# Reordering the expert tiles of a routed MoE stage, with the routing weights' table and the late gate rows moved on TensorE and VectorE

## The chip, the cores and the metric

One Trainium2 chip, one core of it. The metric is the device time of one execution in microseconds. The kernel is one program for one transformer-like layer in 32-bit floats. Its engines are TensorE (PE, with weight loads listed as PEld), VectorE (DVE), ScalarE (ACT), GpSimd (POOL) and SyncE (SP), which only issues DMAs here.

## The reference

640 tokens (512 latent, 128 context) of width 1024 pass through modulation, a gated convolution and a differential attention, a merge with an output projection (result `x`), and then the stage that this case is about:

```python
h2 = rms_norm(x, norm2_g) * (1 + scale2) + shift2
x = x + gate2 * hier_moe(h2, ...)          # gate2 differs for latent and context tokens

def hier_moe(t):                            # 16 experts, each token goes to 2 of them
    for e in range(16):
        he = silu(t @ w1[e]) * (t @ w3[e])  # 1024 -> 512, twice
        y = y + combine[:, e:e + 1] * (he @ w2[e])   # 512 -> 1024
    return y
```

`combine` holds the two routing weights of each token (a softmax over its two experts, times its group's probability).

## The kernel before

Each expert's three matrices (w1 "gate", w3 "up", w2 "down") are 2 MB each, so 48 loads of 2 MB pass through the core once. The experts are sorted on the chip by how many tokens they have. Rank r of that order is read by SP with `expert_at(r)`. Slots for the sorted tokens are packed in twelve output tiles of 128 rows:

- A **couple** t (0 to 5, `t < WHOLE`) joins a large expert `a` (rank 7 - t, 96 rows) with a small expert `b` (rank 8 + t, 32 rows). Its main tile needs both experts' matrices: TensorE works in four strips of 32 rows, three with a's matrix and one with b's.
- Tiles t = 6 and 7 are whole tiles: 128 rows of one large expert (rank 1 and rank 0), so they need only a's matrices.
- A **half tile** holds 64 more rows of one small expert `b`. Two of them (for t = 2j and 2j + 1) make output tile `half j`. So there are 8 half-tile gate/up steps (`half_gate_up`) and 4 joint down steps (`half_down`).

For every main tile TensorE runs `main_gate`, `main_up`, `half_gate_up`, then three blocks of transposes (`hidden_T`, `next_tokens`, `half_hidden_T`) and `main_down`; after an odd t also `next_tokens` and `half_down`. The order of the twelve outputs before is: 0, 1, half 0, 2, 3, half 1, 4, 5, half 2, 6, half 3, 7. In the tail half_down(3) stands behind five of the eight steps of tile 7's gate product.

In the traces these are the lines L2428 (gate and up of a couple), L2430 (of a whole tile), L2452 and L2453 (gate/up of a half tile), L2490 and L2492 (down of a couple and of a whole tile), L2504 (down of a half tile), L2462 (`hidden_T`), L2394 (`next_tokens`) and L2470 (`half_hidden_T`).

The engines pass the work on with semaphores, and every order is written out by hand:

- SP loads matrices into six gate/up buffers and three down buffers (`GU_UNIT`, `DOWN_UNIT`), in the order of the tiles. Before it loads over a buffer it waits for the product that read it (`s_gate_mm`, `s_up_mm`, `s_half_mm`, `s_d`).
- POOL gathers the tokens of the next tiles from `h2` in device memory (three buffers), and adds finished rows onto `y_sample` and `y_prompt` in device memory. A couple's tile and a joint half tile take two such adds each (their strips have rows in common), a whole tile takes one. Each add waits for the one before it.
- ACT copies transposes out of PSUM and computes silu. `tokens_T` copies a tile's transposed tokens.
- DVE multiplies silu by up and by the slot's routing weight (`hidden`, `hidden_half`), makes the row gates of an output tile (`slot_gates(n)`, into one of two buffers `gated`) and multiplies the down product by them (`rows_made(n)`). `slot_gates(n)` waits until the adds of outputs up to n - 2 have landed. Before the change it stands directly behind `rows_made(n - 1)`, which is ahead of the next `hidden`.

Work that leads into the stage: the last tile's h2 is written to device memory by ACT's queue, the slots' token numbers come from `table(i)` on TensorE, the slots' routing weights from `weight_table(i)` (five token tiles, L2406, each needs two one-hot blocks made by DVE), and the last modulation product (`ada_part(LAST_PAIR, ...)`, 8 steps) gives gate2: its product is copied by ACT (`late_rows`), transposed by TensorE (L2509), corrected by DVE, transposed once more (L2517), stored by ACT's queue and read back by POOL's queue as rows `gate2`. DVE turns those into a difference with `gate_difference` (L1874) before the first `slot_gates`.

```python
def slot_gates(n, tile):
    if n >= 2:
        added = 16 * sum(adds_before[m] for m in range(n - 1))
        dve.wait_ge(s_put_lat, added)
        dve.wait_ge(s_put_ctx, added)
```

Of the kernel before, what the change touches and what calls it, by code (L numbers as in the profile page):

```python
# [7 lines left out]
P = 128  # L8
# [214 lines left out]
TOKEN_TILES = [col for t in range(COUPLES) for col in ((t,) if t % 2 else (t, COUPLES + t // 2))]  # L223
XG = 3


def out_main(t):

    return t + t // 2 if t + 1 < COUPLES else TILES - 1


def out_half(j):

    return 3 * j + 2 if j + 1 < QUADS else TILES - 2


def gate_up_units():

    unit = {}
    for t in range(COUPLES):  # L240
        unit[("gate", "a", t)] = unit[("gate", "b", t - 2)] if t >= 2 else 4 * t
        unit[("gate", "b", t)] = unit[("up", "b", t - 2)] if t >= 2 else 4 * t + 1
        unit[("up", "a", t)] = unit[("gate", "a", t - 1)] if t else 2
        unit[("up", "b", t)] = unit[("up", "a", t - 1)] if t else 3
    return unit


def down_units():

    unit = {("a", 0): 0, ("b", 0): 1, ("a", 1): 2, ("b", 1): 0}  # L250
    for t in range(2, COUPLES):
        first, second = (("b", "a") if t + 1 == COUPLES else ("a", "b"))
        unit[(first, t)] = unit[("a", t - 1)] if t % 2 == 0 else unit[("b", t - 2)]
        unit[(second, t)] = unit[("b", t - 2)] if t % 2 == 0 else unit[("a", t - 1)]
    return unit
# [3 lines left out]
GU_LOADS = [(part, which, t) for t in range(COUPLES)  # L259
            for part, which in ((("gate", "b"), ("gate", "a"), ("up", "b"), ("up", "a")) if t + 1 == COUPLES  # L260
                                else (("gate", "a"), ("gate", "b"), ("up", "a"), ("up", "b")))]
DOWN_LOADS = [(which, t) for t in range(COUPLES) for which in ("ba" if t + 1 == COUPLES else "ab")]
# [22 lines left out]
def build(nc, io):  # L285
# [4 lines left out]
    with ExitStack() as ctx:  # L290
# [279 lines left out]
        def _(sp):  # L570
# [100 lines left out]
            for t in range(COUPLES - 1):  # L671
                a, b = expert_at(COUPLES - 1 - t), expert_at(COUPLES + t)
                if t == 1:
                    sp.wait_ge(s_late, 1)
                if t >= 2:
                    sp.wait_ge(s_half_mm, t - 1)
                load_gate_up("gate", "a", t, a)
                if t == 0:
                    job_done(sp, "wo", 2 * NT - 1)
                load_gate_up("gate", "b", t, b)  # L680
                if t:
                    sp.wait_ge(s_gate_mm, t)
                load_gate_up("up", "a", t, a)
                if t:
                    sp.wait_ge(s_up_mm, t)
                else:
                    sp.wait_ge(s_xg[0], 16)
                    sp.wait_ge(s_outx, 16 * NT)
                load_gate_up("up", "b", t, b)
                if t == 0:  # L690
                    sp.wait_ge(s_x2, 2 * NT)
                    sp.wait_ge(s_last_scaled, 1)
                elif t == 1:
                    sp.wait_ge(s_wtable, NT)
                elif t % 2:
                    sp.wait_ge(s_d, 2 * out_half(t // 2 - 1) + 2)
                elif t:
                    sp.wait_ge(s_d, 2 * out_main(t - 1) + 2)
                load_down("a", t, a)
                if t % 2:  # L700
                    sp.wait_ge(s_d, 2 * out_main(t - 1) + 2)
                elif t:
                    sp.wait_ge(s_d, 2 * out_half(t // 2 - 1) + 2)
                load_down("b", t, b)
            t = COUPLES - 1
            a, b = expert_at(0), expert_at(EXPERTS - 1)
            sp.wait_ge(s_half_mm, t - 1)
            load_gate_up("gate", "b", t, b)
            load_gate_up("gate", "a", t, a)
            sp.wait_ge(s_up_mm, t)  # L710
            load_gate_up("up", "b", t, b)
            load_gate_up("up", "a", t, a)
            sp.wait_ge(s_d, 2 * out_half(t // 2 - 1) + 2)
            load_down("b", t, b)
            sp.wait_ge(s_d, 2 * out_main(t - 1) + 2)
            load_down("a", t, a)

# [21 lines left out]
        def _(pool):  # L739
# [166 lines left out]
            for t in range(COUPLES - 1):  # L906
                add_main(t)
                gather_next(XG + 2 + out_main(t))
                if t % 2:
                    add_half(t // 2)  # L910
                    gather_next(XG + 2 + out_half(t // 2))
            add_half(QUADS - 1)
            add_main(COUPLES - 1)
# [27 lines left out]
        def _(act):  # L941
# [240 lines left out]
            def hidden_T(n):  # L1182
                act.wait_ge(s_HT, n + 1)
                if n:
                    act.wait_ge(s_d, 2 * out_main(n - 1) + 2)
# [10 lines left out]
            A(late_rows, late_psum, ACT.Copy).then_inc(s_late_rows, 1)  # L1196
            tokens_T(0)
# [4 lines left out]
            A(unused[:, 2:3], ones[:, 0:1], ACT.Silu)  # L1202
            tokens_T(1, half=True)
            for t in range(COUPLES - 2):
                silu_main(t)
                silu_half(t)
                hidden_T(t)
                tokens_T(2 + out_main(t))
                half_hidden_T(t)
                if t % 2:  # L1210
                    tokens_T(2 + out_half(t // 2), half=True)
            t = COUPLES - 2
            silu_main(t)
            silu_half(t)
            hidden_T(t)
            tokens_T(TILES - 1)
            half_hidden_T(t)
# [1419 lines left out]
```

## Time and profile before

| | us |
|---|---|
| median of 3 runs | 1212.82 (1210.62 to 1213.5) |
| profiled execution, its own time | 1208.31 |
| span of the profiled execution | 1206.5 |
| TensorE busy | 1159.9 (96%) |
| VectorE, GpSimd, ScalarE busy | 537.2, 354.2, 226.2 |
| chain that ended last: PE, DMA, DVE | 78%, 14%, 2% of the span |
| DMA | 201.89 MB, mean 167 GB/s over the span |
| 48 expert matrices | 2048 KB each |

The table is of one execution. The span is what the profiler saw between the first and the last instruction. The expert stage is the last quarter of it: the first expert matrix is asked for at about 885 us and the last add lands at 1206. Busy time says which engine works, not which one sets the end. A matmul in 32-bit floats is listed as two instructions.

### The profile page before, as it was taken

What the parts mean: (1) busy time and instruction counts of PE and PEld (TensorE: products, weight loads), DVE (VectorE), ACT (ScalarE), POOL (GpSimd) and SP (SyncE); (2) the same over time, 40 slices, a digit from 0 to 9 for tenths busy, and PEclk for the clock granted to TensorE, in tenths of its full rate; (3) what the DMA queues carried; (4) which work ended last, traced back from release to release, by engine and by line L of the source; (5) the groups of instructions that cost most, each with busy time, mean ns of one, the idle gap of its engine ahead of it and who ended that gap; (6) DMA issues with size and microseconds to landing.
All of it is one profiled execution on the core that took longest, in us unless ns stands there. A gap on an engine that the chain in (4) does not pass through costs nothing.

```text
span 1206.5 us, 14503 instructions
## 1 busy us (share of the span) xinstructions
PE 1159.9 (96%) x5750; PEld 710.2 (59%) x5751; DVE 537.2 (45%) x1045; ACT 226.2 (19%) x478; POOL 354.2 (29%) x289
## 2 busy tenths in 40 slices
PE   4899999999999999999999999999988999999995
PEld 1567677677777777777777777765543333333332
DVE  2553369365596675275324433545583211211121
ACT  3221247322473001100110011002121111111010
POOL 0465600277103233233333333200001123322323
PEclk9999999999999999999999999999987999999999
DMA  9944320022200222222212223541169999999982
GB/s 353 328 150 164 114 79 1 18 71 79 79 1 1 71 70 71 70 70 70 70 70 70 70 70 142 227 170 72 58 251 361 413 407 409 410 401 411 400 321 28
DMA packets 53988, 201.89 MB, mean 167 GB/s; under 512 B 5344, under 2 KB 5920, under 8 KB 47776
## 3 DMA queue, kind: packets, MB, share of 16 engines
q1 hardware_dynamic: 47040, 185.20, 39.6%
q0 software_dynamic: 6272, 14.17, 4.4%
q10 hardware_dynamic: 608, 1.58, 0.3%
q8 instruction: 46, 0.75, 0.2%
q14 instruction: 22, 0.18, 0.0%
HBM read 189.36 MB, written 18.91 MB: 173 GB/s over the span
## 4 chain that ended last, share of the span: by engine, by line
PE 78%; DMA 14%; DVE 2%; issue 1%; ACT 0%; POOLq 0%; POOL 0%; DVEq 0%
PE psum L2252 35%; PE psum L2058 12%; DMA y_sample<-arena,slot_rows 7%; PE psum L2316 6%; PE psum L2160 4%; PE psum L2220 3%; PE psum L2036 3%; DMA y_sample<-arena,slot_rows_b 3%; PE psum L2428 2%; PE psum L1978 2%; PE psum L2452 2%; DMA y_sample<-arena,slot_rows_q 1%; DMA y_prompt<-arena,slot_rows_ctx 1%; PE psum L2194 1%; PE psum L2430 1%
## 5 line engine op out<-in xcount | busy, mean ns | idle before, releaser
L2252 PE MATMUL psum<-arena,weight_ring 128*128 128x320 f32 x928 | 256.9, 432 | 0.0
L2252 PEld LDWEIGHTS psum<-arena,weight_ring 128*128 128x128 f32 x928 | 175.9, 190 | 72.7
L762 POOL TENSOR_TENSOR weight_ring<-weight_ring 128x512 f32<-128x512 f32 x80 | 107.0, 1338 | 352.5 <-DMA weight_ring<-in_w_in 201.4
L2252 PE MATMUL psum<-x,weight_ring 128*128 128x320 f32 x640 | 179.5, 432 | 0.0
L2252 PEld LDWEIGHTS psum<-x,weight_ring 128*128 128x128 f32 x640 | 121.1, 190 | 49.6
L763 POOL TENSOR_TENSOR weight_ring<-weight_ring 128x512 f32<-128x512 f32 x80 | 110.8, 1385 | 0.0
L1537 DVE TENSOR_TENSOR arena<-psum,arena 128x320 f32<-128x320 f32 x124 | 59.5, 488 | 92.1 <-PE psum L2252 91.4
L2058 PE MATMUL psum<-weight_ring,x 128*128 128x256 f32 x384 | 88.3, 380 | 0.5 <-DVE x L1294 0.5
L2428 PE MATMUL psum<-weight_ring,arena 128*32 128x512 f32 x512 | 78.6, 609 | 1.1 <-ACT arena L1167 1.1
L2058 PEld LDWEIGHTS psum<-weight_ring,x 128*128 128x128 f32 x384 | 71.6, 190 | 11.7 <-DVE x L1294 1.3
L2316 PE MATMUL psum<-weight_ring,arena 128*128 128x512 f32 x160 | 71.8, 596 | 0.0
L2058 PE MATMUL psum<-weight_ring,arena 128*128 128x256 f32 x288 | 67.5, 381 | 0.0
L1537 DVE TENSOR_TENSOR arena<-psum,ropeC 128x320 f32<-128x320 f32 x40 | 19.6, 491 | 102.3 <-PE psum L2252 102.0
L1132 ACT ACTIVATE ropeC<-psum 128x320 f32<-128x320 f32 x28 | 12.2, 437 | 263.7 <-PE psum L2252 246.7
L2058 PEld LDWEIGHTS psum<-weight_ring,arena 128*128 128x128 f32 x288 | 53.3, 190 | 10.8 <-issue 4.3
L1905 DVE SCALAR_TENSOR_TENSOR arena<-arena,ropeC 128x1024 f32<-128x1024 f32 x12 | 15.4, 1282 | 84.0 <-DMA y_prompt<-arena,slot_rows_b_ctx 62.8
L1088 ACT ACTIVATE arena<-psum,softmax_stats 128x640 f32<-128x640 f32 x64 | 50.5, 792 | 7.4 <-DVE softmax_stats L1462 7.4
L1462 DVE TENSOR_REDUCE softmax_stats<-psum 128x2 f32<-128x1280 f32 x32 | 47.7, 1490 | 6.6 <-PE psum L2160 6.4
L946 ACT ACTIVATE arena<-psum 128x512 f32<-128x512 f32 (+1 forms) x49 | 26.9, 552 | 122.2 <-PE psum L2073 59.5
L2316 PEld LDWEIGHTS psum<-weight_ring,arena 128*128 128x128 f32 x160 | 29.3, 190 | 31.2 <-issue 31.1
L1913 DVE TENSOR_TENSOR arena<-psum,arena 128x512 f32<-128x512 f32 x24 | 16.5, 691 | 69.3 <-PE psum L2490 36.6
L2160 PE MATMUL psum<-arena 64*128 64x128 f32 (+3 forms) x256 | 46.2, 467 | 0.0
(346 smaller groups left out, 1530.4 us busy)
## 6 DMA issues: line engine op xcount, KB each, us to landing
arena<-in_w SPq DMA_DIRECT2D x22, 2048.0 KB, 17.2
weight_ring<-in_w SPq DMA_DIRECT2D x21, 2048.0 KB, 23.5
weight_ring<-in_w_in SPq DMA_DIRECT2D x16, 2048.0 KB, 8.4
arena<-in_w_ada SPq DMA_DIRECT2D x6, 2048.0 KB, 11.5
x<-in_w SPq DMA_DIRECT2D x5, 2048.0 KB
weight_ring<-in_w_ada SPq DMA_DIRECT2D x8, 1024.0 KB, 14.3
x<-in_x_sample SPq DMA_DIRECT2D x2, 2048.0 KB, 12.2
weight_ring<-in_w_conv_out SPq DMA_DIRECT2D x2, 2048.0 KB, 7.8
```

The costliest lines, as they stand in the source:

```text
L762: nc.gpsimd.tensor_tensor(out[:, 0:2], a_[:, 0:2], b_[:, 0:2], op)
L763: nc.gpsimd.tensor_tensor(out[:, 2:4], a_[:, 2:4], b_[:, 2:4], op).then_inc(signal, 1)
L1088: last = A(prob[n % 2][:, c, :], S[:, KEYS * c:KEYS * (c + 1)], ACT.Exp, bias=st[:, c:c + 1], accum_out=st[:, 4 + c:5 + c])
L1462: V.reduce_max(sm[:, 8 * (n % 4):8 * (n % 4) + 2], S2, axis=AX, negate=True).then_inc(s_max, 1)
L1537: return V.tensor_tensor(out, product_psum(q, name), value, add)
L2036: last = mm(ps[LANE * half:LANE * (half + 1), 0:512], hT[:, k, HALF * half:HALF * half + LANE], w, start=(k == 0), stop=(k == KT - 1))
L2058: last = mm(ps[:, 0:256], x_[:, k, :], w_[:, k, :], start=(k == 0), stop=(k == 3))
L2160: last = mm(psum[:, base + KEYS * c + lo:base + KEYS * c + hi], q, kT[64 * c:64 * (c + 1), h, key:key + hi - lo], start=True, stop=True)
L2220: last = mm(psum[:, lo:lo + P], aT[n % 2][:, P * j:P * (j + 1)], v_sb[:, j, P * h:P * (h + 1)], start=(j == 0), stop=(j == NT - 1))
L2252: last = mm(product_psum(q, name), w[:, k, :], src[:, k, :], start=(k == 0), stop=(k == 3))
L2316: last = mm(ps[:, 0:512], mixT[:, k, P * i:P * (i + 1)], w[:, k, :], start=(k == 0), stop=(k == KT - 1))
L2428: last = mm(out[rows_, :], xgT[:, k, rows_], (b if lane == 3 else a)[:, k, :], start=(k == 0), stop=(k == KT - 1))
```

## The change

It changes orders, and with them the counts that the semaphores wait for. No product and no load is added or dropped.

- **Tiles.** Tile 6 (`FIRST`, the whole tile of rank 1) goes first, without its half tile. Then the couples 0 to 5. Then `half_gate_up(6)`, `half_down(2)`, `main_down(5)`, `half_gate_up(7)`, and tile 7 (`LAST`), with half_down(3) now behind three of the eight steps of its gate product. Outputs: 6, 0, 1, half 0, 2, 3, half 1, 4, half 2, 5, half 3, 7. `before(t)` is the place of main tile t in this order.
- **Loads.** Only gate a, up a and down a of tile 6 come before the first tokens are gathered (before: gate a, gate b, up a of couple 0). The six of couple 0 follow. At the end come gate b and up b of 6 and 7, gate a and up a of 7, then the down matrices b6, b7, a7; both b7 and a7 wait for `main_down(5)`.
- **Ahead of the first tokens.** The late modulation product is cut: steps 2 to 4 before `table`, 5 to 7 behind it. All five `weight_table` blocks stand ahead of the first tokens' transposes. The late product's first transposes stand behind tile 6's gate product, its second behind two steps of the up product; DVE does its part after the expert counts.
- **Gate rows.** `gate_difference` and `slot_gates(0)` stand behind couple 0's `hidden_half`; every later `slot_gates(n)` directly ahead of its own `rows_made(n)`, and for a main tile behind that couple's `hidden_half`.

```diff
+FIRST, LAST = COUPLES - 2, COUPLES - 1
+MAINS = [FIRST] + list(range(WHOLE)) + [LAST]
+TOKEN_TILES = [FIRST, 0, COUPLES, 1, 2, COUPLES + 1, 3, 4, COUPLES + 2, 5, LAST, COUPLES + 3]
+OUT_TILES = [FIRST, 0, 1, COUPLES, 2, 3, COUPLES + 1, 4, COUPLES + 2, 5, COUPLES + 3, LAST]
...
+            load_gate_up("gate", "a", FIRST, first)
+            job_done(sp, "wo", 2 * NT - 1)
+            load_gate_up("up", "a", FIRST, first)
+            sp.wait_ge(s_x2, 2 * NT)
+            sp.wait_ge(s_last_scaled, 1)
+            load_down("a", FIRST, first)
...
+            t = WHOLE - 1
+            sp.wait_ge(s_half_mm, t)
+            load_gate_up("gate", "b", FIRST, small)
+            load_gate_up("up", "b", FIRST, small)
...
+            sp.wait_ge(s_d, 2 * out_half(t // 2) + 2)
+            load_down("b", FIRST, small)
+            sp.wait_ge(s_d, 2 * out_main(t) + 2)
+            load_down("b", LAST, b)
+            load_down("a", LAST, a)
...
@@ DVE
+            hidden(FIRST)
             hidden(0)
             hidden_half(0)
             gate_difference()
-            slot_gates(0, 0)
+            slot_gates(0)
             rows_made(0)
-            slot_gates(1, 1)
...
+            for t in range(WHOLE):
+                if t:
+                    hidden(t)
+                    hidden_half(t)
+                if t + 1 < WHOLE:
+                    slot_gates(out_main(t))
+                    rows_made(out_main(t))
+                    if t % 2:
+                        slot_gates(out_half(t // 2))
+                        rows_made(out_half(t // 2))
...
@@ TensorE
-            ada_part(LAST_PAIR, late_psum, range(2, 8), late_slot).then_inc(s_late, 1)
+            ada_part(LAST_PAIR, late_psum, range(2, 5), late_slot)
             for i in range(NT):
                 table(i)
+            ada_part(LAST_PAIR, late_psum, range(5, 8), late_slot).then_inc(s_late, 1)
...
+            pe.wait_ge(s_order, 1)
+            weight_table(range(NT))
+            next_tokens(0)
+            main_gate(FIRST)
             pe.wait_ge(s_late_rows, 1)
             for t in range(4):
                 last = tr(late_T_psum[:, P * t:P * (t + 1)], late_rows[:, P * t:P * (t + 1)], ident[:, :])
             last.then_inc(s_lateT, 1)
-            pe.wait_ge(s_order, 1)
-            weight_table(range(2))
-            next_tokens(0)
-            main_gate(0)
-            weight_table(range(2, NT))
...
+            main_part(FIRST, "up", up_psum, range(0, 2))
+            pe.wait_ge(s_late_mod, 1)
+            tr(late_rows_psum[0:16, 0:P], rowpack[:, 48:64], ident[:, :]).then_inc(s_late_packT, 1)
+            main_part(FIRST, "up", up_psum, range(2, KT)).then_inc(s_up_mm, 1)
             next_tokens(1)
...
+            hidden_T(FIRST)
+            main_gate(0)
             pe.wait_ge(s_late_copied, 1)
             pe.wait_ge(s_shifted, 1)
-            main_down(0)
...
+            main_down(FIRST)
+            next_tokens(2)
+            for t in range(WHOLE):
+                if t:
+                    main_gate(t)
+                main_up(t)
+                half_gate_up(t)
+                hidden_T(t)
+                next_tokens(3 + t + t // 2)
+                half_hidden_T(t)
+                if t + 1 < WHOLE:
+                    main_down(t)
+                    if t % 2:
+                        next_tokens(5 + 3 * (t // 2))
+                        half_down(t // 2)
+            t = WHOLE - 1
+            next_tokens(5 + 3 * (t // 2))
+            half_gate_up(FIRST)
+            half_down(t // 2)
+            half_hidden_T(FIRST)
+            main_down(t)
+            half_gate_up(LAST)
...
+            main_part(LAST, "gate", gate_psum, range(0, 2))
+            half_hidden_T(LAST)
+            main_part(LAST, "gate", gate_psum, range(2, 3))
             half_down(QUADS - 1)
-            main_part(t, "gate", gate_psum, range(5, KT)).then_inc(s_gate_mm, 1)
...
+            main_part(LAST, "gate", gate_psum, range(3, KT)).then_inc(s_gate_mm, 1)
```

## Rows read from the trace of the kernel before

**Rows 1.** Busy time by stretch: length, then PE, PEld, DVE, ACT, POOL, PEclk, DMA share, GB/s

```profile
910.00:1171.00 261.00, 256.69 (x1743) 94.47 (x1745) 45.89 (x81) 29.24 (x45) 67.86 (x49) 0.99 1.01 404
```

**Rows 2.** TensorE's waits, 905 to 1206 us: total, times, longest

```profile
PE psum L2462 <- DVE arena L1883: 3.2, 3, 1.6
```

**Rows 3.** Chain that ended last, the way into the stage: start, length, what

```profile
894.06 11.16 DMA h_scratch<-arena
...
910.33 1.99 PE psum L2394 x8
912.34 1.03 ACT arena L1167
913.41 8.97 PE psum L2428 x64
922.38 0.83 PE psum L2406 x4
...
925.34 0.16 PE psum L2519 x2
...
925.70 1.09 PE psum L2394 x8
```

**Rows 4.** The same chain, couple 1

```profile
950.00 13.73 PE psum L2428 x128
963.73 0.57 PE psum L2452
...
970.75 0.68 PE psum L2462 x4
...
972.94 7.05 PE psum L2490 x64
```

**Rows 5.** The same chain, the tail

```profile
1169.35 7.02 PE psum L2504 x32
1176.37 9.65 PE psum L2430 x22
```

**Rows 6.** DVE in order of time: start, us, line, shapes, idle before

```profile
948.62 1.22 DVE L1874 TENSOR_TENSOR arena<-arena 128x1024 f32<-128x1024 f32 x1 [6.39 <-DMA arena<-rows_scratch]
...
951.20 1.29 DVE L1913 TENSOR_TENSOR arena<-psum,arena 128x512 f32<-128x512 f32 x2
...
971.42 0.76 DVE L1891 SCALAR_TENSOR_TENSOR slot_one_hots<-psum,ropeC,ropeS 64x512 f32<-64x512 f32 x1 [6.87 <-ACT ropeS L1180]
...
1145.69 1.28 DVE L1905 SCALAR_TENSOR_TENSOR arena<-arena,ropeC 128x1024 f32<-128x1024 f32 x1 [19.77 <-DMA y_prompt<-arena,slot_rows_b_ctx]
...
1195.46 0.69 DVE L1913 TENSOR_TENSOR arena<-psum,arena 128x512 f32<-128x512 f32 x1 [2.67 <-PE psum L2492]
```

**Rows 7.** SP's queue in order of time, the stage's fourth load and its last two

```profile
910.30 0.33 SPq L659 DMA_DIRECT2D x<-in_w  x1
...
1140.04 17.35 SPq L663 DMA_DIRECT2D arena<-in_w  x2
```

**Rows 8.** The last load, issued at 1157 us: KB, us from issue to landing

```profile
arena<-in_w SPq DMA_DIRECT2D x1, 2048.0 KB, 16.7
```

**Rows 9.** All gate and up loads (issued on L659), from issue to landing

```profile
DMA to landing us min/median/max: 7.6/23.5/27.8
```

**Rows 10.** All down loads (issued on L663), from issue to landing

```profile
DMA to landing us min/median/max: 12.9/17.2/28.1
```

**Rows 11.** POOL's adds in order of time

```profile
981.50 1.73 POOL L868 DMA_INDIRECT y_sample<-arena,slot_rows  x1 [6.74 <-DVE arena L1913]
...
1183.07 1.42 POOL L868 DMA_INDIRECT y_sample<-arena,slot_rows_q  x1 [1.74 <-DMA y_sample<-arena,slot_rows]
...
1196.93 1.57 POOL L868 DMA_INDIRECT y_sample<-arena,slot_rows  x1 [10.72 <-DVE arena L1913]
```

**Rows 12.** TensorE's clock (the last column but two) in two stretches

```profile
914.00:916.00 2.00, 2.00 (x16) 0.42 (x12) 0.00 (x0) 0.00 (x0) 0.00 (x0) 0.50 1.01 414
...
918.00:920.00 2.00, 2.00 (x24) 0.52 (x20) 0.00 (x0) 0.00 (x0) 0.00 (x0) 1.00 0.94 393
```

More of the change, by code:

```diff
@@ L232, in out_half @@
 def out_half(j):
-    return 3 * j + 2 if j + 1 < QUADS else TILES - 2
+    return OUT_TILES.index(COUPLES + j)
 def gate_up_units():
[L239 to L244, printed above, removed]
+    unit = {("gate", "a", FIRST): 0, ("up", "a", FIRST): 1, ("gate", "a", 0): 2, ("gate", "b", 0): 3, ("up", "a", 0): 4, ("up", "b", 0): 5}
@@ L245, in gate_up_units @@
+    unit[("gate", "a", LAST)], unit[("up", "a", LAST)] = unit[("gate", "b", t)], unit[("up", "b", t)]
     return unit
 def down_units():
[L250 to L254, printed above, removed]
+    unit = {("a", FIRST): 0, ("a", 0): 1, ("b", 0): 2, ("a", 1): 0, ("b", 1): 1}
@@ L255, in down_units @@
+    for t in range(2, WHOLE):
+        unit[("a", t)] = unit[("a", t - 1)] if t % 2 == 0 else unit[("b", t - 2)]
+        unit[("b", t)] = unit[("b", t - 2)] if t % 2 == 0 else unit[("a", t - 1)]
+    t = WHOLE - 1
+    unit[("b", FIRST)], unit[("b", LAST)], unit[("a", LAST)] = unit[("b", t - 1)], unit[("b", t)], unit[("a", t)]
     return unit
 GU_UNIT, DOWN_UNIT = gate_up_units(), down_units()
-GU_LOADS = [(part, which, t) for t in range(COUPLES)
-            for part, which in ((("gate", "b"), ("gate", "a"), ("up", "b"), ("up", "a")) if t + 1 == COUPLES
-                                else (("gate", "a"), ("gate", "b"), ("up", "a"), ("up", "b")))]
@@ L262 @@
-DOWN_LOADS = [(which, t) for t in range(COUPLES) for which in ("ba" if t + 1 == COUPLES else "ab")]
+GU_LOADS = ([("gate", "a", FIRST), ("up", "a", FIRST)]
+            + [(part, which, t) for t in range(WHOLE) for part in ("gate", "up") for which in "ab"]
+            + [(part, which, t) for which, t in (("b", FIRST), ("b", LAST), ("a", LAST)) for part in ("gate", "up")])
+DOWN_LOADS = [("a", FIRST)] + [(which, t) for t in range(WHOLE) for which in "ab"] + [("b", FIRST), ("b", LAST), ("a", LAST)]
@@ L670, in _ @@
             sp.wait_ge(s_order, 1)
[L671 to L675, printed above, removed]
+            first = expert_at(LAST - FIRST)
+            load_gate_up("gate", "a", FIRST, first)
[5 more added lines that the diff above has]
+            for t in range(WHOLE):
+                a, b = expert_at(LAST - t), expert_at(COUPLES + t)
+                if t == 0:
+                    sp.wait_ge(s_xg[0], 16)
+                elif t == 1:
+                    sp.wait_ge(s_gate_mm, before(FIRST) + 1)
+                else:
                     sp.wait_ge(s_half_mm, t - 1)
@@ L704, in _ @@
                 load_down("b", t, b)
[L705 to L715, printed above, removed]
@@ L904, in add_half @@
                 add_rows(out_half(j), LANE, P, idx_q[0:LANE, j:j + 1], idx_q_ctx[0:LANE, j:j + 1])
[L906 to L913, printed above, removed]
+            for n, tile in enumerate(OUT_TILES):
+                if tile < COUPLES:
+                    add_main(tile)
+                else:
+                    add_half(tile - COUPLES)
+                gather_next(XG + 2 + n)
             copies = steps[0]
@@ L1898, in _, with slot_gates @@
                 adds_before[out_half(j)] = 2
-            def slot_gates(n, tile):
+            def slot_gates(n):
+                tile = OUT_TILES[n]
                 if n >= 2:
```

197 lines of the change are left out of this document (93 added, 104 removed).

## Prediction

> **What bounds the kernel now.** I read the busy time by stretch first. Only orders in and around the expert stage change, so the question is which engine fills it. From 910 to 1171 us both do: TensorE is busy for 256.7 of 261 us and the 16 DMA engines show a share of 1.01 [rows 1]. The share cannot say which one sets the end, so I went on to the waits. TensorE never waits for a matrix. In the body of the stage it waits for DVE's `hidden`, three times, 3.2 us in all [rows 2]. One of the three is the last tile's own hidden product, about 0.8 (the DVE operation of that kind takes 0.76 [rows 6]); nothing can be put in its place. The other 2.4 us come from the adds: `slot_gates` stands ahead of the next `hidden` and at 1145.69 it has waited 19.8 us for rows to land in `y_prompt` [rows 6]. Then the chain at both ends. The way in is h2's last write, 11.16 us from 894.06, then the gather, then transposes at 910.33, ACT's copy and the first product at 913.41 [rows 3]. TensorE's order from there to the last rows at 1195.46 [rows 6] is a plain sum of blocks, so a change of order can be costed block by block.
>
> **Blocks.** Gate and up of a couple take 13.73, so 6.9 each; the half tile's product runs from 963.73 to 970.75, 7.0; the three blocks of transposes end at 972.94, 2.2; a down product takes 7.05 [rows 4]. A whole tile's are as long: 11 steps in 9.65, 0.88 a step [rows 5], 7.0 for eight.
>
> **Ahead of the stage.** The gather waits for h2's last write. Three loads stand ahead of that write before and after, so I leave 910.33 where it is; down a6 is issued some microseconds later than up a of couple 0 was, but two loads are enough to keep the DMA engines in work till then. Three of the five weight-table blocks, 922.38 to 925.34, move into the wait for the gather: -3.0. With that cover gone they would cost what they cost now. The late product's first transposes move the other way, from that wait to behind tile 6's gate: four transposes of 128 columns, like `hidden_T`'s 0.68 [rows 4], so +0.7. What follows from 925.34 to 925.70 [rows 3] stays on the path. SP reads one expert number less before its first load; I count it as nothing.
>
> **Tile 6 first.** The seam behind it has no half tile. `main_gate(0)` needs ACT's copy of the tokens' transposes, 1.03 [rows 3], and only `hidden_T`, 0.68, lies beside it: with 0.1 for the signal +0.45.
>
> **Gate rows late.** The DVE order puts `gate_difference`, `slot_gates(0)` and the first half of `rows_made(0)` behind couple 0's `hidden_half`. That product starts 0.67 after the half tile's end and lasts 0.76 [rows 4, 6], so DVE is free at +1.43. From the start of `gate_difference`, 948.62, to the first half of the rows, 951.20 + 0.69 (the last row's length for such a half), are 3.3 [rows 6]: done at +4.8. TensorE is ready for `main_down(0)` at +2.2 [rows 4], and that product takes the banks which `rows_made(0)` empties. It waits 2.6 us. Before, this work lay beside products: bounds 0 (if it were still hidden) and 4.8 - 2.2 = 2.6; the DVE order leaves no way to hide it, so +2.6. In exchange `slot_gates(n)` no longer blocks a `hidden` and has one output more of slack: -2.4. Is that slack enough? Adds pass at (1145.7 - 981.5)/7 = 23.5 us an output [rows 6, 11]. After, output 6's single add starts near 968 and takes about half of that, couple 0's start near 982, and every later `slot_gates` finds its adds landed by 3 to 20 us. Yes.
>
> **Tail.** `half_gate_up(6)` needs the tokens transposed just ahead of it. The block itself waits for the copy of tile 7's tokens (1.03 + 0.05 less the 0.62 of the half tile's transposes, the four that end the 2.2 of rows 4): 0.45; then its own copy is bare, 1.1. Before, `half_down` lay beside both. +1.55.
>
> TensorE's own sum: -3.0 - 2.4 + 0.7 + 0.45 + 2.6 + 1.55 = -0.1.
>
> **The loads.** Now the other engine. From 910.30 [rows 7] to the last landing at 1157.06 + 16.7 = 1173.8 [rows 7, 8] are 263.5 us for 45 loads, 5.86 each. They are as many after. What changes is how far they run ahead. With the blocks above couple 1's gate starts at 973.3 instead of 950.0 [rows 4], 23.3 later, and only three loads, 17.6 us, are put ahead of it. So at each release of a buffer SP's queue holds 5.7 us less. Before, the shortest landing of a down load is 12.9 [rows 10] against 7.6 for a load into an almost empty queue [rows 9]: 5.3 us of work ahead of it. After, about none, so the DMA engines run dry for a moment where two releases lie far apart (down a2, then b2 behind `half_down(0)`). No product waits there, its matrices are 10 us early. At the end it counts. `half_down(3)` needs down b7, which is issued when `main_down(5)` ends and `half_gate_up(7)` begins. Before, that product begins at about 1157.3: 1169.35 less five gate steps of 0.88, 0.6 of transposes and 7.0 [rows 4, 5]. After, 0.1 earlier, 1157.2, and b7 is issued then instead of at 1140.04 [rows 7]. With the shortest landing, 12.9 [rows 10], it is there at 1170.1. TensorE comes to `half_down(3)` two gate steps earlier than before: 1169.35 - 0.1 - 1.75 = 1167.5. So it waits 2.6 us. From below: 7.6 [rows 9] gives 1164.8, no wait. From above: the median, 17.2 [rows 10], gives 1174.4, a wait of 6.9. I take 12.9, since one load (b6, issued 7 us before) and some of the rest are still ahead of it.
>
> Sum: -0.1 + 2.6 = **+2.5 us**. Against the profiled execution's 1208.31 (span 1206.5, 1.8 around it) that is 1210.8. The three runs lie at 1212.82 in the median, 4.5 above the profiled one; 1212.82 + 2.5 = **1215.3**. The bound of "no change" is 0.3%, 3.6 us.
>
> **The clock.** The first product ran at half clock: 0.50 from 914 to 916, 1.00 from 918 [rows 12], and took 8.97 instead of 6.9, the transposes before it 1.99 instead of 1.09 [rows 3]. Together 3.0 us. After, more of TensorE's work lies just ahead of 910 (weight tables, late steps), and if the clock were at its upper level there, 3.0 would be gained. But ACT's copy, 1.03, still stands between. The Trainium skill, "TensorE: Matmul & The Clock Gate", Part 1, says that the throttled state is the default and that sustained activity releases it. By that rule the fuller stretch speaks for this gain, and the sum would be -0.5 instead of +2.5, if the loads let it.
>
> **The rivals.**
>
> *A, the loads fall further behind, slower.* b7 lands as late as the median says, or SP's queue has run dry more than once. The wait is 6.9 instead of 2.6: +6.8, or 1219.6. For it: b7 and a7 are now issued together, 17 us later than b7 was, and gate b6 and up b6, which `half_gate_up(6)` needs, wait for `main_down(4)`. Against it: fewer adds have passed by then, so the same engines have less to move. It decides from a b7 landing later than 1171.2 (a wait above 3.7).
>
> *B, TensorE's gains stay, faster.* The unprofiled runs are 4.5 us longer than the profiled one, and I can't see where. If that time lies in `hidden` waits behind the adds, the removed wait is 6.9 and not 2.4. With b7 in time: -0.1 - 4.5 = -4.6, or 1208.2. With the clock up as well 3 more. Against it: a slower DMA also delays b7, and `half_down(3)` then takes the gain back.
>
> *C, the adds set the end.* The last add can't start before half 3's two have landed. They can't start before 1175, and couple 5's must be through. Before: 6 us each once the loads are over (1177 to 1183.07), and the last add at 1196.93 waited for its rows alone [rows 11]. After, output half 2's adds start only at 1150 and couple 5's near 1170: half 3's end at 1194 to 1197. That is 0 to 3 us of delay; at worst +5.3, 1218.
>
> *D, nothing moves.* Waits traded for waits in equal size, b7 just in time: -0.1, 1212.7.
>
> **How the numbers follow.** My forecast, the sum with a small wait for b7: 0.42. D: 0.16. A 0.20, C at its worst 0.07, B 0.10, the clock's gain with b7 in time 0.05 (-3.1 and less). The range reaches from the clock's case, 1209.5, to A and a little over, 1220; it leaves out B and A's far end. Faster by over 0.3%: B and a part of the clock's case, 0.13. Slower by over 0.3%: A, C and the upper end of my own case, 0.30. The rest 0.57.
>
> **What would show it.** After: no L2406 between the first gate and up product; a wait of about 2.6 us at the first L2490 of couple 0 for DVE's rows; `hidden` never late; a wait of 1 to 1.5 us at the first `half_gate_up` of the tail for ACT's copy; a wait at the last L2504 for a DMA, or none; DMA share under 1 near 1005 to 1015; the last add waiting for its rows alone. I am wrong if the first gather lands at another time (the loads ahead of h2's write), if matrices are waited for in the middle, or if the last wait is over 4 us.

## The result and the profile after

| | before | after |
|---|---|---|
| median of 20 runs | 1209.14 (1206.66 to 1213.5) | 1212.82 (1209.17 to 1216.64) |
| profiled execution, its own time | 1208.31 | 1213.2 |
| its span | 1206.5 | 1211.4 |
| ratio of the runs | | 1.0025, interval 1.0017 to 1.0033 |

By the ratio of the runs the change made the kernel slower by 3.0 us (2.1 to 4.0); the two medians alone are 3.7 apart. The prediction's sum was +2.5, with "within 0.3%" as the likeliest class. The loss is smaller than that bound, but 20 runs on each side resolve it, so it is a small loss and not no change. The 1212.82 now measured is inside the range; that it is closer to the old median of before than to my 1215.3 comes from that median, which was high: 1212.82 in three runs, 1209.14 in twenty.

Of the 4.9 us between the two spans, 2.1 lie ahead of the first tokens' gather: h2's last write starts at 896.15 instead of 894.06 [rows 3]. From that write to the start of the last rows operation before takes 1195.46 - 894.06 = 301.4 us [rows 3, 6], after 1200.14 - 896.15 = 304.0. So this stretch is 2.6 longer in these two executions.

Busy time of after in the stretch of [rows 1], the same columns:

```profile
910.00:1171.00 261.00, 254.16 (x1733) 94.21 (x1733) 46.11 (x88) 28.00 (x44) 60.64 (x47) 0.98 1.00 401
```

TensorE has 2.5 us more of idle time, and the clock's mean went from 0.99 to 0.98. TensorE's waits of after in the stage (total, times, longest):

```profile
PE psum L2524 <- DVE arena L1941: 2.6, 1, 2.6
PE psum L2486 <- DMA x<-in_w: 1.9, 1, 1.9
PE psum L2462 <- ACT arena L1193: 1.1, 1, 1.1
PE psum L2496 <- DVE arena L1910: 0.8, 1, 0.8
PE psum L2438 <- DVE arena L1805: 0.7, 2, 0.5
```

L2496 is `hidden_T`: of its three waits [rows 2] the last tile's is left, which nothing can hide; 2.4 us are gone, as forecast. L2524 is couple 0's down product, which waits for `rows_made(0)`: 2.6, as forecast. The one that I did not have is L2486, `half_gate_up(6)`, which waits for a matrix. The chain that ended last, the way in and couple 0 (start, length, what):

```profile
912.24 0.89 PE psum L2438 x4
913.13 0.89 PE psum L2426 x8
914.04 1.03 ACT arena L1193
...
915.12 7.13 PE psum L2462 x16
922.25 0.44 PE psum L2547 x4
...
962.67 1.14 DVE arena L1900
963.84 1.30 DVE arena L1933
965.16 0.70 DVE arena L1941
...
966.00 8.54 PE psum L2524 x64
974.54 5.55 PE psum L2460 x49
```

The weight tables (L2438) run until 913.13, 0.7 longer than the gather would have needed by the distance of before (896.15 + 910.33 - 894.06 = 912.42 [rows 3]). So TensorE does not wait for the gather at all, only 1.1 for ACT's copy, and the first product takes 7.13 instead of 8.97 [rows 3]. After the 2.6 us for DVE's rows the down product takes 8.54 instead of 7.05 [rows 4]. The same chain at the tail:

```profile
1113.88 23.22 DMA x<-in_w
1137.24 1.09 PE psum L2486
1138.36 0.82 PE psum L2486
...
1143.35 0.41 PE psum L2486
...
1147.21 6.87 PE psum L2538 x32
...
1172.31 7.02 PE psum L2538 x32
1179.33 11.37 PE psum L2462 x26
```

Up b6 is issued at 1113.88 and lands 23.2 us later. TensorE has stood since 1135.39; ACT's copy was ready near 1136.5, so the load adds 0.7 to the 1.1 that I had for the copy. Then each step of the half tile's product takes 0.82 instead of 0.41 until 1143. The product ends at 1147.21, 9.97 us after it began, instead of 7.0. The rows by stretch (columns as in [rows 1]) show why: TensorE's clock, the last column but two, is at 0.50 in the third of them.

```profile
1134.00:1136.00 2.00, 1.15 (x8) 0.95 (x8) 0.00 (x0) 1.04 (x3) 1.07 (x1) 1.00 1.01 422
1136.00:1138.00 2.00, 0.76 (x2) 0.32 (x4) 0.00 (x0) 0.45 (x1) 0.27 (x1) 0.57 1.00 426
1138.00:1140.00 2.00, 2.00 (x8) 0.70 (x6) 0.00 (x0) 0.00 (x0) 1.03 (x1) 0.50 1.09 385
1142.00:1144.00 2.00, 2.00 (x8) 0.57 (x6) 0.00 (x0) 0.00 (x0) 0.00 (x0) 0.73 1.06 451
```

So the balance of the stretch from h2's write, each term from the rows above against those of before:

| term | forecast | measured |
|---|---|---|
| h2's write to the first product (tables, transposes) | 0 | -0.4 |
| first product at the full clock | 0 (rival: -2.1 of its -3.0) | -1.8 |
| weight table behind the first product | -3.0 | -3.0 |
| late product's transposes (L2547) | +0.7 | +0.4 |
| copy at `main_gate(0)` | +0.45 | +0.3 |
| `hidden` | -2.4 | -2.4 |
| rows of output 0 late | +2.6 | +2.6 |
| half clock behind it | not in the sum | +1.5 |
| `half_gate_up(6)`: block's copy, own copy | +0.45 +1.1 | +0.5 +1.1 |
| its matrix up b6 | not in the sum | +0.7 |
| half clock behind it | not in the sum | +3.0 |
| down b7 at `half_down(3)` | +2.6 | 0 |
| sum | +2.5 | +2.5 |

The measured terms give 2.5 of the 2.6. That the forecast's sum is the same is luck: terms that it did not have come to +3.0 (-0.4 - 1.8 + 1.5 + 0.7 + 3.0), the +2.6 that it had for b7 was not paid, and small differences make the last -0.4. The table is of one execution each, and its two half-clock terms are not the same in every execution: behind the same wait of 2.6 at couple 0, e1 lost 2.9 and e2 nothing. The adds did not set the end; POOL's last ones, with what it waited for in brackets:

```profile
1189.42 1.40 POOL L896 DMA_INDIRECT y_sample<-arena,slot_rows_q  x1 [1.80 <-DMA y_sample<-arena,slot_rows]
...
1201.61 1.57 POOL L896 DMA_INDIRECT y_sample<-arena,slot_rows  x1 [9.09 <-DVE arena L1941]
```

### The profile page after: what moved, and what is told of

It is laid out like the page before. It is cut to its first block, busy times and chain, and to the rows that moved or that the text cites. A ratio compares the mean times of both kernels' runs of the same rounds, so it can differ in the third digit from the quotient of the medians.

```text
span 1211.4 us, 14502 instructions
## 1 busy us (share of the span) xinstructions
PE 1163.2 (96%) x5750; PEld 710.6 (59%) x5751; DVE 532.8 (44%) x1045; ACT 226.3 (19%) x478; POOL 348.7 (29%) x289
## 4 chain that ended last, share of the span: by engine, by line
PE 92%; DMA 3%; DVE 2%; ACT 1%; issue 0%; SPq 0%; POOLq 0%; POOL 0%; DVEq 0%
PE psum L2283 35%; PE psum L2089 12%; PE psum L2460 6%; PE psum L2347 6%; PE psum L2486 4%; PE psum L2067 4%; PE psum L2191 4%; PE psum L2524 4%; PE psum L2009 3%; PE psum L2251 3%; PE psum L2462 2%; PE psum L2538 2%; DMA x<-in_w 2%; PE psum L2225 1%; PE psum L2526 1%; DMA weight_ring<-in_w_ada 1%
## 5 line engine op out<-in xcount | busy, mean ns | idle before, releaser
L1910 DVE SCALAR_TENSOR_TENSOR arena<-psum,ropeC,arena 128x512 f32<-128x512 f32 x8 | 6.0, 751 | 106.2 <-PE psum L2460 88.7
L2067 PE MATMUL psum<-weight_ring,arena 128*64 128x512 f32 x192 | 45.6, 629 | 2.7 <-ACT arena L983 2.7
L2524 PE MATMUL psum<-arena 128*32 128x512 f32 x384 | 43.9, 610 | 2.6 <-DVE arena L1941 2.6
```

Of the source, the lines that this page charges most:

```text
L2067: last = mm(ps[LANE * half:LANE * (half + 1), 0:512], hT[:, k, HALF * half:HALF * half + LANE], w, start=(k == 0), stop=(k == KT - 1))
L2524: last = mm(out[rows_, :], hhT[:, k, rows_], (b if lane == 3 else a)[:, k, cols_], start=(k == 0), stop=(k == 3))
```

## Experiments

Two theories were tested. Theory L: TensorE and the DMA engines are both full, tile 6 first costs one load's time (5.7 us by the prediction's sum) of lead, and whatever TensorE gains is handed over to the next matrix that lands late: up b6 at `half_gate_up(6)`, or down b7 at `half_down(3)`. Its rival S: TensorE's own stops set the end; at `half_gate_up(6)` the bare copy alone stops TensorE and drops the clock. Line names below: L2486 (L2490 in two kernels) half tile's gate and up, L2538 (L2542) half tile's down, L2524 (L2528) a couple's down. "Stage" in the table is the time from the start of the first tokens' transposes to the start of the last rows operation in the profiled execution; it was 285.1 before and 287.2 after.

| run | ratio to before, interval | median | stage | wait for a matrix |
|---|---|---|---|---|
| after | 1.0025, 1.0017 to 1.0033 | 1212.82 | 287.2 | up b6 1.9 (0.7 beyond the copy) |
| e1 | 1.0003, 0.9988 to 1.0017 | 1210.36 | 287.7 | b7 0.9 |
| e2 | 1.0020, 1.0004 to 1.0037 | 1213.94 | 285.9 | b7 1.6 |
| e3 | 1.0011, 0.9999 to 1.0024 | 1212.09 | 287.4 | up b6 5.4, and 1.1 |
| e4 | 1.0023, 1.0011 to 1.0035 | 1213.36 | 287.5 | b7 4.1 |
| e5 | 0.9991, 0.9978 to 1.0003 | 1208.69 | 283.7 | 0.4 and 0.4 |
| e6 | 1.0005, 0.9996 to 1.0015 | 1209.55 | 282.1 | 2.8 in three |
| e7 | 1.0084, 1.0066 to 1.0101 | 1219.57 | 292.0 | up b6 1.6 |
| e9 | 0.9982, 0.9972 to 0.9991 | 1207.63 | 282.6 | none |
| e11 | 0.9960, 0.9946 to 0.9974 | 1204.60 | 281.4 | none |
| e10 | 0.9972, 0.9962 to 0.9983 | 1206.64 | 281.4 | 1.7 |
| e8 | 0.9992, 0.9981 to 1.0003 | 1208.74 | 284.3 | 5.7 in five |

The stages are of single executions, swing by the clock, as the last section shows, and start later where tables stand ahead of the tokens (e6, e8 and those from after). The ratios carry the verdicts. Each is against runs of the kernel before taken beside it.

**e1, the small expert's gate and up loads ahead of down b5.**

```diff
-                load_down("b", t, b)
+                if t + 1 < WHOLE:
+                    load_down("b", t, b)
...
             sp.wait_ge(s_half_mm, t)
             load_gate_up("gate", "b", FIRST, small)
             load_gate_up("up", "b", FIRST, small)
+            sp.wait_ge(s_d, 2 * out_main(t - 1) + 2)
+            load_down("b", t, b)
```

> The changed kernel, with gate b6 and up b6 asked for ahead of down b5 (as soon as half_gate_up(4) has freed their buffers, about 11 us earlier); nothing else. In the changed kernel's trace half_gate_up(6) starts 1.85 us after its tokens' transposes: 1.1 us of that is ACT's copy, the last 0.7 us is up b6 landing, and the product then runs its first seven steps at half clock (10.0 us instead of 7.0). Theory L (the loads): the landing is what stops TensorE and lets the clock fall; both go, -3.7 us against the changed kernel, a ratio to the kernel before near 0.9995. Theory S (the seam): the bare copy alone is stop enough, the clock falls all the same; -0.7 us, ratio near 1.002. If L is right the trace shows no wait for a matrix and a half_gate_up(6) of 7.0 us.

2.7 us less than after in the ratios; the two intervals just touch. `half_gate_up(6)` waits 1.1 for its copy alone and then takes 7.0: a stop of 1.1 did not drop the clock, which speaks against S. The load that comes late is now the next one (chain of e1):

```profile
1158.88 11.20 DMA arena<-in_w
...
1170.32 7.09 PE psum L2542 x32
```

**e2, `half_down(2)` ahead of `half_gate_up(6)`**, where it hides the copy, with DVE's rows in that order too.

```diff
             next_tokens(5 + 3 * (t // 2))
+            half_down(t // 2)
             half_gate_up(FIRST)
-            half_down(t // 2)
```

> The changed kernel, with half_down(2) ahead of half_gate_up(6) on TensorE (and the rows of half 2 ahead of hidden_half(6) on DVE). The half tile's down product then covers both ACT's copy and 7 us of the landing of up b6. Both theories expect the stop and the half clock gone: -1.1 - 0.7 - 3.0 = -4.8 us against the changed kernel, ratio to the kernel before near 0.9985. If the time does not fall by more than 1 us, the tail is bound by something else (the loads for tile 7, or the adds), and the trace shows a new wait at half_down(3) or ahead of the last add.

The stop at `half_gate_up(6)` and its half clock are gone, 4.8 us, and by the ratios the time did not move beyond the noise (1.0020 against 1.0025). Two things take the gain. The edit itself makes a new stop: `half_hidden_T(6)` now stands directly behind `half_gate_up(6)`, with no product between them, and waits 1.5 for DVE:

```profile
PE psum L2504 <- DVE slot_one_hots L1918: 1.5, 1, 1.5
```

That stop is in e4, e9 and e11 too, which have this order. And TensorE comes to `half_down(3)` sooner and waits there, 1.6, and the half clock follows (chain of e2; 8.76 instead of 7.0):

```profile
1155.84 11.91 DMA arena<-in_w
...
1167.99 8.76 PE psum L2538 x32
```

**e3, couple 0's gate rows ahead of its `hidden`**, which takes the 2.6 us wait away.

```diff
             hidden(FIRST)
-            hidden(0)
-            hidden_half(0)
             gate_difference()
             slot_gates(0)
             rows_made(0)
+            hidden(0)
+            hidden_half(0)
```

> The changed kernel, with gate_difference, slot_gates(0) and rows_made(0) back ahead of hidden(0), beside couple 0's up product; nothing else. The wait of 2.6 us at main_down(0) goes. Theory L (the DMA engines set the end through up b6): TensorE arrives 2.6 us earlier at half_gate_up(6) and waits 2.6 us longer for the load; the time stays, ratio 1.0025, and the wait for the matrix grows from 1.9 to about 4.5 us. Theory S (TensorE's own seams set the end): -2.6 us, ratio near 1.0003. In between if releases of buffers, and so the loads, move up with TensorE.

Couple 0's down product waits for nothing and takes 7.0, so TensorE has 2.6 + 1.5 = 4.1 us in hand at 970. It gives back 1.1 at a matrix in the body and 3.5 at up b6 (5.4 instead of 1.9); the half clock behind it costs 2.3 instead of 3.0, and the stage is as long as after's (287.4 and 287.2). e3's waits:

```profile
PE psum L2486 <- DMA x<-in_w: 5.4, 1, 5.4
PE psum L2460 <- DMA weight_ring<-in_w: 1.1, 1, 1.1
```

Up b6 itself, from the chain of e3:

```profile
1109.87 28.12 DMA x<-in_w
```

It was issued 4.0 us earlier than in the changed kernel (1113.88) and landed at 1138.0, not earlier than there (1137.1). This is theory L in one run: 4.1 us of TensorE's time taken away are worth 1.7 in the ratios, with intervals that overlap.

**e4, e2 and e3 together** (their two diffs).

> e2's and e3's edits together. If the two losses are separate and the loads leave room: -4.8 - 2.6 = -7.4 us against the changed kernel, ratio to the kernel before near 0.9964, faster than both kernels. If the DMA engines set the end once the seams are gone: only -4.8 or a little more, ratio 0.998 to 0.9985, with a wait for up b6 or for down b7 of 1 to 3 us in the trace.

Both gains in one kernel, with e2's new stop of 1.5: 1.0023. b7's wait is 4.1 and the half clock behind it costs 1.8 (chain of e4):

```profile
1154.26 14.39 DMA arena<-in_w
...
1168.93 8.79 PE psum L2538 x32
```

**e5, the kernel before with each `slot_gates` directly ahead of its own `rows_made`.** It leaves the old tiles.

```diff
             rows_made(0)
-            slot_gates(1, 1)
...
                 n = out_main(t)
+                slot_gates(n, t)
                 rows_made(n)
                 if t % 2:
                     slot_gates(n + 1, COUPLES + t // 2)
                     rows_made(n + 1)
-                    slot_gates(n + 2, t + 1)
-                elif t < COUPLES - 2:
-                    slot_gates(n + 1, t + 1)
```

> The kernel before, with one part of the change alone: for t of 1 and more, slot_gates(n) stands directly ahead of its own rows_made(n), behind the couple's hidden and hidden_half. Theory P (as predicted): the 2.4 us that hidden waited for the adds go, TensorE arrives earlier, ratio near 0.998. Theory L (the DMA engines set the end through down b7): in the kernel before b7 is issued at 1140 and needed at 1169.35; TensorE's gain is mostly kept only if b7 has landed; otherwise a wait for a matrix of 1 to 2 us shows at half_down(3) and the ratio is 0.999 to 1.0.

The two `hidden` waits are gone. The time is lower by 0.9 parts in a thousand with an interval that reaches 1.0003; the 2.4 us that were expected would be 2.0 parts. Two small waits for a matrix, 0.4 each, are new.

**e6, the kernel before with the weight tables ahead of the first tokens and the late product split.**

```diff
-            ada_part(LAST_PAIR, late_psum, range(2, 8), late_slot).then_inc(s_late, 1)
+            ada_part(LAST_PAIR, late_psum, range(2, 5), late_slot)
             for i in range(NT):
                 table(i)
+            ada_part(LAST_PAIR, late_psum, range(5, 8), late_slot).then_inc(s_late, 1)
...
-            weight_table(range(2))
+            weight_table(range(NT))
             next_tokens(0)
             main_gate(0)
-            weight_table(range(2, NT))
```

> The kernel before, with the other part alone: late modulation product cut in two, all five weight_table blocks ahead of the first tokens, the late transposes behind couple 0's gate product and inside its up product. As predicted: -3.0 + 0.7 = -2.3 us, ratio near 0.998. With the clock at its upper level at the first product (the changed kernel's trace shows a first product of 7.1 us where the kernel before has 9.0) up to 3.0 more, 0.9956. Theory L: down b7 lands no earlier, so a wait for a matrix at half_down(3) takes back 1 to 2 us; ratio 0.999.

It gave nothing, where 2.3 us were expected (the interval leaves that out). In the profiled execution the first product takes 7.07 and no table stands behind it, but h2's last write starts at 896.02, 2.0 later than before, and from that write to the last rows e6 needs 300.5 us, only 0.9 less than before. TensorE's waits of e6: new ones for a matrix (a third is 0.3), and `hidden` still late:

```profile
PE psum L2429 <- DMA weight_ring<-in_w: 2.5, 2, 1.4
PE psum L2463 <- DVE arena L1883: 1.6, 3, 0.8
```

**e7, after with three of the weight-table blocks back behind tile 6's gate product.**

```diff
-            weight_table(range(NT))
+            weight_table(range(2))
             next_tokens(0)
             main_gate(FIRST)
+            weight_table(range(2, NT))
```

> The changed kernel, with three of the five weight_table blocks back behind the first gate product (tile 6's). TensorE's sum: +3.0 us. Theory L (up b6's landing sets the tail): TensorE comes 3.0 us later to half_gate_up(6), up b6 has landed by then, the stop is the copy's 1.1 us alone; only 1 to 2 us of the 3.0 reach the end, ratio to the kernel before 1.0025 to 1.004. Theory S (TensorE's seams set the end): all of it, ratio 1.005.

7.1 us over after, where 3.0 were expected. The trace has the rest:

```profile
PE psum L2555 <- DVE rowpack L1890: 3.2, 1, 3.2
```

DVE's late part stands behind the expert counts, and those wait for the tables, so the transposes of `rowpack` wait 3.2 us; the up product behind them takes 6.55 for its last 12 instructions instead of 5.15. 2.7 + 3.2 + 1.4 = 7.3. The tables ahead of the tokens are thus needed by the rest of the change. The sum is as large as the loss in the ratios, but this one execution won something back: `half_gate_up(6)` waited 1.6 and then ran at the full clock, where after lost 3.0. The execution is 2.7 below e7's median.

This run came out against what I had written for theory L, that up b6 would have landed when TensorE comes late. Up b6 was issued 7.0 us later than in the changed kernel, at 1120.85, because SP holds it and the loads ahead of it back until TensorE has done `main_down(4)`, and it landed 22.95 us later, so the wait was still there. So a loss of TensorE that lies ahead of the loads' issue was paid in full here, while the gain of e3 was handed over.

**e9, e4 with `half_down(3)` behind tile 7's whole gate product.** If L holds, b7 needs time and not a faster TensorE.

```diff
             half_hidden_T(LAST)
-            main_part(LAST, "gate", gate_psum, range(2, 3))
+            main_part(LAST, "gate", gate_psum, range(2, KT)).then_inc(s_gate_mm, 1)
             half_down(QUADS - 1)
-            main_part(LAST, "gate", gate_psum, range(3, KT)).then_inc(s_gate_mm, 1)
```

> The last kernel of the first four (half_down(2) ahead of half_gate_up(6), first gate rows early), and now half_down(3) behind tile 7's whole gate product instead of behind three of its eight steps, 4.4 us later. Its predecessor waits 4.1 us at half_down(3) for down b7 and then runs it at half clock (8.8 us instead of 7.0). Theory L: both go, -5.9 us against it, ratio to the kernel before 0.997 to 0.998, no wait for a matrix left, the last add still waits for its rows alone. Rival C (the adds set the end): half 3's rows come up to 0.5 us later than before and its adds end later than tile 7's rows; the last add then waits for an add, and the gain stays under 3 us.

Faster than both kernels: 1.8 parts in a thousand below before, 4.3 below after. Nothing waits for a matrix. The two down loads land 12.7 and 17.8 us after they were issued at 1156.4 and 1156.8, the first at 1169.1 at the soonest, and TensorE comes to it at 1171.25 (chain of e9):

```profile
1171.25 7.02 PE psum L2538 x32
1178.27 7.08 PE psum L2462 x16
```

**e11, e4 with every add cut to its first 16 rows.** Most of the output rows are left out; all instructions and waits stay.

```diff
+                hi, lat, ctx_ = lo + 16, lat[0:16, :], ctx_[0:16, :]
```

> e4_down_first_rows_early with every add into the output cut to its first 16 rows (all instructions, waits and semaphores stay; most of the output rows are left out). Theory L (the 4.1 us wait of half_down(3) is for a matrix that comes late because the DMA engines are full, adds included): with about an eighth of the add traffic the loads land sooner, the wait is under 1 us or gone, half_down(3) runs in 7.0 us at the full clock in place of 8.8, and no other wait for a matrix appears; the time is 4 to 8 us below e4's 1213.4, so 1205 to 1209, ratio to before 0.994 to 0.999. Rival B (the wait comes from when the buffer is freed and the load issued, adds don't matter): the wait stays at 3.5 to 4.5 us and the time within 1.5 us of 1213.4.

The wait of 4.1 is gone, and the time is 6.3 parts in a thousand, 7.6 us, below e4's. POOL's queue, which carries the adds and the gathers, fell from this in e4 (packets, MB, share of 16 engines)

```profile
q0 software_dynamic: 6272, 14.17, 4.4%
```

to this in e11:

```profile
q0 software_dynamic: 3904, 10.36, 2.7%
```

and the loads into `weight_ring` land in 18.2 us in the median instead of 23.1. So the matrix of e4 is late in part because the adds slow the loads down. Whether they meet at the 16 DMA engines or at the memory behind them, e11 does not tell. The Trainium skill, "DMA: Bandwidth & Descriptors", section "Queues, rings and completion order", has each DMA engine take packets from its queue rows in turn. The trace agrees as far as that taking 1.7% of the span from the small queue shortened the big one's median landing by 5 us; no run here shows the taking of turns itself.

**e10, e4's gate rows, e1's loads and e9's place for `half_down(3)`.** `half_gate_up(6)` keeps the changed kernel's place. The edits are those of e3, e1 and e9.

> The changed kernel with three edits together: the couple's gate rows made first (as e3_gate_rows_early), the small expert's gate and up loads ahead of the couple's second down load (as e1_small_loads_early), half_down(3) behind the whole gate product of tile 7 (as e9_half3_behind_gate). It differs from e9 in that half_gate_up(6) keeps its place. Theory L: the same slack is made in another way, so no wait for a matrix over 0.5 us is left and the time is that of e9, 1206.5 to 1208.5, ratio 0.997 to 0.999. Rival: the early small loads put down b5 or b6 late in place of b7 (one of them is queued behind them), a wait of 1 to 3 us at half_down(2) or main_down(5) with its half clock, 1210 to 1213, ratio 1.001 to 1.003.

Of the kernels that compute everything it has the lowest ratio, though its interval overlaps e9's: 2.8 parts in a thousand (3.4 us) below before, 5.3 below after. I had expected no matrix wait over 0.5. There is one of 1.7, before couple 5's up product, and no half clock behind it (TensorE in order of time):

```profile
1115.67 7.07 PE L2464 MATMUL psum<-weight_ring,arena 128*32 128x512 f32 x64 [1.73 <-DMA weight_ring<-in_w]
```

**e8, the kernel before with e5 and e6 together**: the whole change but the order of the tiles and of their loads.

> The kernel before with the change's other parts and the old tile order: weight tables ahead of the first tokens, late product split, each slot_gates directly ahead of its own rows_made. Theory L: without the early small tile nothing is taken from the loads' lead, but nothing more than e5 and e6 gave either, 1207.5 to 1209.5, ratio 0.9985 to 1.000; waits for a load of 0.5 to 2.5 us at the couples take what hidden's 2.4 us gave. Rival T (the table and gate parts themselves cost, not the tile order): 1211 to 1213, ratio 1.0015 to 1.003.

0.9992. Neither clearly a gain nor a loss, against 1.0025 for the whole change. The two intervals lie apart. So the loss belongs to the new order of tiles, with its loads and its stops (no run has that order alone), and the other parts are worth at most 2.3 us on the old order. e8 waits in five places for matrices, 5.7 us in all.

## Why the prediction was right and where it was wrong

*Right.* No table block stands between the first products, -3.0. `hidden` is never late. The forecast that every `slot_gates` finds its adds landed 3 to 20 us early did not hold for two of them, which waited for adds (2.47 us at 1007.72 and 5.75 at 1175.90), but TensorE waited for neither. 2.6 at couple 0's down product, to a tenth. The copies of the tail, 1.6. The last add waits for its rows alone, so rival C is out. The DMA share falls under 1 near 1005 (0.97 from 1000 to 1010). And the kind of loss behind the forecast's sign: a matrix comes late near the end, where none did before. That the lead is smaller by 5.7 us was not measured.

*Wrong, the place.* The step "it waits 2.6 us" at `half_down(3)` failed. In the changed kernel b7 is issued at 1161.8, not 1157.2: 2.1 of the 4.6 lie ahead of the stage (h2's last write, which the prediction had left at its old time), and the rest is what TensorE lost at couple 0's half clock and at `half_gate_up(6)` beyond the forecast, less what the first product gave. The two loads of that moment land 7.9 and 13.3 us later, and `half_down(3)` starts at 1172.31 without a wait. The matrix that was late stood one product earlier. I had named gate b6 and up b6 in rival A and not worked them out, though [rows 9] had the number: with the issue at 1113.9, as the changed kernel's trace has it (3 us behind the end of `main_down(4)`), plus the median of 23.5, it lands at 1137.4, and the half tile was ready for it at 1136.5. e1 shows that with up b6 early b7 is indeed the next one late.

*Wrong, what a stop costs.* A stop was priced at its length. The runs often show more: 2.6 us at couple 0's down product and 1.5 behind it (2.9 in e1, 1.7 in e7, nothing in e2); 1.9 at `half_gate_up(6)` and 3.0 behind it (nothing behind 1.6 in e7); 1.6 or 4.1 at `half_down(3)` and 1.7 or 1.8 behind it. The two that fell into the changed kernel's execution, 4.5 us, are larger than the whole loss, and they hid behind the -1.8 of the first product, which I had given a chance of 0.05 with its 3.0.

*The class.* With a sum of +2.5 I had put most of the chance on "within 0.3%"; three runs of before spread over 2.9 us. The measured 0.25% is inside that bound and still a loss that 20 runs resolve. The bound was too wide for it.

*Rival A* had named the loads that came late, but its price, 6.9 at b7, was not paid in any kernel; 4.1 in e4 is the most. *Rival D* (waits for waits in equal size) describes e3 and e4 better than the changed kernel. Rival B's unseen `hidden` waits were not there: e5 removed them all and gained 1.1 us, interval -0.4 to 2.7, not 6.9.

Three things stay open. The first is what of e5's and e8's gains is real, as their intervals do not exclude 1. The second is why e9's gain over e4 (5 us) is nearly as large as wait and half clock together (5.9), while e3's is less than half of its own. The third is whether the 2.1 us ahead of the stage belong to the change. h2's last write starts at 894.06 in both kernels that leave the late modulation product whole (before and e5). Of the eleven that cut it in two, nine have it at 895.6 to 896.5, and two (e1 and e4) at 893.9 and 894.2. That speaks for the cut product, or what moved with it, as a cost that the prediction put at nothing, but each is one execution, and no run tests it alone.

## What to carry to other kernels

Where the loads are as full as the engine they feed, the order of products is a question of when each matrix lands. List for each product the issue of its load plus the usual time to landing against the time at which the engine gets there, for every product near the end and not for the last one alone. A gain on the engine is kept only if it does not reach the next of these dates: here 4.1 us saved early came back as 4.6 of waiting, while moving one product of 7 us behind work whose matrices had landed gave 5. And price a stop as a range, from its length alone to its length and the 1.4 to 3.0 us that a fallen clock cost behind it here.

## What the runs showed of the hardware

After some stops in mid-stage TensorE's clock fell to its lower level (granted 0.50, which is 1.2 of 2.4 GHz) by the start of the next product or just behind it, and was back at 1.00 some 3 to 6 us of work later. The length of the stop alone did not decide it. The clock fell behind stops of 1.6 (e2), 1.9 (after), 2.5 or 2.6 (after, e1, e7), 3.2 (e7), 4.1 (e4) and 5.4 us (e3). It did not fall behind any mid-stage stop of 1.5 or less, nor behind 1.6 at `half_gate_up(6)` in e7 and at `hidden_T` in the kernel before, 1.7 in e10, 1.8 and 1.9 in e8 and 2.6 at couple 0's down product in e2. That last stop is the same one in e1 and e2, and the product behind it took 9.93 in e1 and 7.07 in e2 (TensorE in order of time, e1, then e2):

```profile
965.37 9.93 PE L2528 MATMUL psum<-arena 128*32 128x512 f32 x64 [2.55 <-DVE arena L1945]
964.79 7.07 PE L2524 MATMUL psum<-arena 128*32 128x512 f32 x64 [2.56 <-DVE arena L1941]
```

The Trainium skill, "TensorE: Matmul & The Clock Gate", Part 1, has activity release the throttle and idleness bring it back. The traces agree with the direction. In them stops of 1.6 to 2.6 us went either way.

The first product seems to be the same matter. In these thirteen executions its clock goes with how long TensorE stood waiting for the gather just ahead of its transposes. It took 8.6 to 9.0 us where that wait was 1.2 to 2.1 (before, e1, e4, e9, e11), and 7.1 where it was 1.0 or less (e2 0.75, e8 0.86, e7 1.00, and after, e3, e6 and e10 with none); e5, with 0.26 there but 1.80 ahead of the table block before it, took 8.96. So in these executions the tables ahead of the tokens gave the clock back only where they ran until shortly before the gather landed, and that was worth 1.8 us. It may be a part of the spread of 7.5 us in the 20 runs of after; the runs without a profile don't show it.
